# Banded attention in two halves of the heads, with the gate's second half computed between its steps

## The reference

```python
def swa_sink_mixer(x, ln_g, w_in, q_norm_g, sinks, w_out, k_band, v_band, cos, sin):
    h = rmsnorm(x, ln_g)
    q, z = jnp.split(h @ w_in, 2, axis=-1)
    q = partial_rope(rmsnorm(q.reshape(bsz, seq, N_HEADS, HEAD_DIM), q_norm_g), cos, sin)
    ...
    def block_attn(args):                 # one block of 128 queries, keys of it and of the block before
        s = jnp.einsum("bqkgd,bckd->bkgqc", qb, kb) * scale
        s = jnp.where(mask[None, None, None], s, NEG_INF)
        m = jnp.maximum(jnp.max(s, axis=-1, keepdims=True), sink)
        p = jnp.exp(s - m)
        denom = jnp.sum(p, axis=-1, keepdims=True) + jnp.exp(sink - m)
        return jnp.einsum("bkgqc,bckd->bqkgd", p / denom, vb)
    o = lax.map(block_attn, (q, k_band, v_band, jnp.arange(nb)))
    return (o * jax.nn.silu(z)) @ w_out
```

## Time and profile before

| | us |
|---|---|
| median of 3 runs | 1655.44 (1652.76 to 1659.08) |
| the profiled execution | 1645.69, its span 1643.8 |
| PE busy, share of the span | 1356.7, 83% |
| DVE, ACT, POOL busy | 574.7, 416.2, 383.4 |
| mean granted TensorE clock | 0.917 |

### The profile page before, as it was taken

The page is one execution under the profiler, slowest core; times in us unless marked ns, Lnnn a source line. Parts: engine busy times, 40 slices in busy tenths (PEclk is TensorE's granted clock), DMA queues, the critical chain, the costliest instruction groups (busy, mean ns, idle before and its releaser), DMA issues. The chain is left out here.

```text
span 1643.8 us, 16317 instructions
## 1 busy us (share of the span) xinstructions
PE 1356.7 (83%) x6188; PEld 902.0 (55%) x6188; DVE 574.7 (35%) x1069; ACT 416.2 (25%) x787; POOL 383.4 (23%) x241
## 2 busy tenths in 40 slices
PE   3998777698978957968887788783499999999698
PEld 2776554488854753323332333231488887788366
DVE  3749755814024151211111111113531323554652
ACT  4323243415332110000000000002423222433541
POOL 5423222024640012111111111105043432000231
PEclk9999898799989958988998999897799999999799
DMA  7121111223320484999999999997023221332000
GB/s 190 52 103 51 52 52 51 78 77 129 129 76 4 170 341 171 381 409 392 412 407 401 409 377 415 402 413 277 8 95 103 102 94 60 103 102 78 26 20 33
DMA packets 71149, 297.70 MB, mean 181 GB/s; under 512 B 9080, under 2 KB 9128, under 8 KB 50352
## 3 DMA queue, kind: packets, MB, share of 16 engines
q1 hardware_dynamic: 63696, 282.27, 44.6%
q0 software_dynamic: 7392, 14.59, 2.7%
HBM read 292.63 MB, written 12.58 MB: 186 GB/s over the span
## 5 line engine op out<-in xcount | busy, mean ns | idle before, releaser
L688 POOL TENSOR_TENSOR ring_rounded<-ring,ring_rounded 128x2048 fp32r<-128x2048 f32 x54 | 253.3, 4706 | 420.1 <-ACT ring_rounded L1297 419.9
L1033 PE MATMUL bank<-ring,B 128*64 128x512 f32 x992 | 251.4, 665 | 84.5 <-DMA ring<-in_w 83.6
L803 PE MATMUL bank<-HT_rounded,ring_rounded 128*128 128x512 f32 x544 | 217.8, 400 | 5.9 <-DVE ring_rounded L1648 3.3
L805 PE MATMUL bank<-HT_rounded,ring_rounded 128*128 128x512 f32 x544 | 213.6, 393 | 0.0
L804 PE MATMUL bank<-ring_rounded 128*128 128x512 f32 x544 | 213.4, 392 | 0.0
L1033 PEld LDWEIGHTS bank<-ring,B 128*64 128x64 f32 x992 | 85.9, 153 | 226.9 <-issue 225.4
L2000 DVE TENSOR_TENSOR B<-bank,small 128x512 f32<-128x512 f32 x32 | 22.1, 691 | 354.2 <-PE bank L1025 354.2
L1297 ACT ACTIVATE ring_rounded<-ring 128x2048 fp32r<-128x2048 f32 x58 | 110.3, 1915 | 121.5 <-DMA ring<-in_w_in_a 50.6
L805 PE MATMUL bank<-ring_rounded 128*128 128x512 f32 x352 | 138.1, 392 | 0.0
L803 PEld LDWEIGHTS bank<-HT_rounded,ring_rounded 128*128 128x128 f32 x544 | 103.4, 190 | 35.6 <-issue 7.6
L804 PEld LDWEIGHTS bank<-ring_rounded 128*128 128x128 f32 x544 | 103.4, 190 | 22.2 <-issue 1.4
(11 more groups left out here) (355 smaller groups left out, 1917.1 us busy)
## 6 DMA issues: line engine op xcount, KB each, us to landing
ring<-in_w SPq DMA_DIRECT2D x77, 2048.0 KB, 14.9
A<-in_w SPq DMA_DIRECT2D x17, 2048.0 KB, 8.4
ring<-in_w_in_a SPq DMA_DIRECT2D x16, 1024.0 KB, 5.1
ring<-in_w_in SPq DMA_DIRECT2D x14, 1024.0 KB, 7.4
ring<-in_w_in_b SPq DMA_DIRECT2D x8, 1024.0 KB, 5.4
ring<-in_w_out SPq DMA_DIRECT2D x4, 1024.0 KB, 6.2
ring<-in_w_xk SPq DMA_DIRECT2D x4, 1024.0 KB, 5.1
ring<-in_w_xv SPq DMA_DIRECT2D x4, 1024.0 KB, 5.2
```

Of the source, the lines that this page charges most:

```text
L688: pool.tensor_tensor(r32(lo), lo, r32_read(quarter(g, True)), ALU.subtract).then_inc(w_split, 1)
L803: pe.matmul(o, r32(a_hi), r32(b_hi), start=first, stop=False)
L805: return pe.matmul(o, r32(a_lo), r32(b_hi), start=False, stop=last)
L1033: last = pe.matmul(bank[2 + b][64 * j:64 * j + 64, :], xgT[b][:, k, hf, :], w, start=(n == 0), stop=(n == 7), skip_group_check=True)
```

## The change

- The pairs are taken in another order: `window_of(i)` gives the groups 0 and 1 of all four query blocks in steps 0 to 7, groups 2 and 3 in steps 8 to 15.
- zz 4 to 7 leave their place ahead of the loop. One is computed at the end of steps 0, 2, 4 and 6 (`GATE_AT`). Its Silu becomes four operations: ScalarE exp(-z) one step later, behind that step's exponentials; GpSimd adds 1; VectorE, at the head of step i + 2, takes the reciprocal and multiplies by z. That product empties the bank.
- All output blocks come at steps 14 to 18 (one a step) and three after the loop; the last two are computed together in three parts of their rows.
- The splitting of wb1 moves from steps 2 and 3 to 9 and 10, and the chunk zz1 is counted as read when zz 7 is filled.
- The probabilities of the first eight steps lie in other buffers, since hT and lowT are read by zz 4 to 7 until step 6. The low halves of groups 0 and 1 lie in B2.
- The counts of emptied banks follow a list of their own (`emptied`), since VectorE no longer empties in TensorE's order.

```diff
-    uses("act", [("zz", m) for m in range(4, 8)])
+    before = len(closed)
     for i in range(16 + 3):
         if i < 16:
             uses("act", [("ws", i, 0), ("ws", i, 1)])
...
         if i >= 3:
             uses("dve", [("wv", i - 3)])
+        if i in GATE_AT:
+            uses("dve", [("zz", GATE_AT[i])])
         if i in OUT_AT:
             uses("dve", [("wb",) + OUT_AT[i]])
-    uses("dve", [("wb", n, NT - 1) for n in range(2)])
-    return opened, closed, by
-
-
-OUT_AT = {8: (0, 0), 10: (1, 0), 12: (0, 1), 14: (1, 1), 16: (0, 2), 18: (1, 2)}
+    uses("dve", [("wb", 1, 2), ("wb", 0, 3), ("wb", 1, 3)])
+    emptied = closed[:before]
+    for i in range(16 + 4):
+        if i < 16:
+            emptied += [("ws", i, 0), ("ws", i, 1)]
+        if i - 1 in OUT_AT:
+            emptied.append(("wb",) + OUT_AT[i - 1])
+        if i - 2 in GATE_AT:
+            emptied.append(("zz", GATE_AT[i - 2]))
+        if 2 <= i < 18:
+            emptied += [("wp", i - 2, kt) for kt in window_tiles(i - 2)]
+        if 3 <= i < 19:
+            emptied.append(("wv", i - 3))
+    emptied += [("wb", 1, 2), ("wb", 0, 3), ("wb", 1, 3)]
+    return opened, closed, emptied, by
+
+
+GATE_AT = {0: 4, 2: 5, 4: 6, 6: 7}
+OUT_AT = {14: (0, 0), 15: (1, 0), 16: (0, 1), 17: (1, 1), 18: (0, 2)}
+
+
+def window_of(i):
+
+    if i < 8:
+        return i // 2, i % 2
+    return i // 2 - 4, 2 + i % 2
...
-            add_chunk(f"zz{n}", w_cols(w_b, D + 512 * n), V, ("zz", 4 * n + 3))
+            add_chunk(f"zz{n}", w_cols(w_b, D + 512 * n), V, ("zz", 4 * n + 3), n == 0)
...
+                if j in GATE_AT:
+                    m = GATE_AT[j]
+                    pool.wait_ge(sem("z_exp_ready"), m - 3)
+                    pool.tensor_scalar(zT[:, m, :], zT[:, m, :], 1.0, None, ALU.add).then_inc(sem("z_sum_ready"), 1)
...
-            to_cols("zz1", V, [("zz", m) for m in range(4, 8)], hT, lowT)
...
+                if i in GATE_AT:
+                    m = GATE_AT[i]
+                    w = chunk("zz1")
+                    split_gemm(fill(V, "zz", m)[:, :], lambda k: w(k, P * (m - 4), P * (m - 3)), cols)
                 if i in OUT_AT:
                     out_block(*OUT_AT[i])
-            for n in range(2):
-                out_block(n, NT - 1)
+            out_block(1, 2)
+            outs = [fill(V, "wb", n, NT - 1)[:, :] for n in range(2)]
+            parts = [chunk(f"wb{n}") for n in range(2)]
+            for k0, k1, rows in ((0, 4, 8), (4, 6, 15), (6, 8, 16)):
+                pe.wait_ge(sem("y3_low_ready"), rows)
...
-            for m in range(4, 8):
-                o = filled(V["zz", m])
-                act.activation(zT[:, m, :], o[:, :], ACT.Silu).then_inc(done, 1)
...
+                if i - 1 in GATE_AT:
+                    m = GATE_AT[i - 1]
+                    o = filled(V["zz", m])
+                    act.activation(zT[:, m, :], o[:, :], ACT.Exp, scale=-1.0).then_inc(sem("z_exp_ready"), 1)
+                if i in (9, 10):
+                    high_half("wb1", i - 9)
...
+                if i - 2 in GATE_AT:
+                    m = GATE_AT[i - 2]
+                    o = filled(V["zz", m])
+                    dve.wait_ge(sem("z_sum_ready"), m - 3)
+                    own(dve.reciprocal(zT[:, m, :], zT[:, m, :]))
+                    dve.tensor_tensor(zT[:, m, :], o[:, :], zT[:, m, :], ALU.mult).then_inc(done, 1)
```

More of the change, by code:

```diff
@@ L177, in second_plan @@
     opened, by = [what for what, _ in plan], dict(plan)
-    closed = list(opened)
+    closed, emptied = list(opened), []
     def uses(engine, whats, opens=True, closes=True):
@@ L234, in __init__, with number @@
         self.emptied = of_engine
-def number(opened, closed, by, base, act0, dve0):
-    assert sorted(map(str, opened)) == sorted(map(str, closed))
+def number(opened, closed, order, by, base, act0, dve0):
+    assert sorted(map(str, opened)) == sorted(map(str, closed)) == sorted(map(str, order))
     count, emptied = {"act": act0, "dve": dve0}, {}
-    for what in closed:
+    for what in order:
         count[by[what]] += 1
@@ L266, in build @@
     order1 = [what for what, _ in plan1]
-    U, act1, dve1 = number(order1, order1, dict(plan1), 0, 0, 0)
+    U, act1, dve1 = number(order1, order1, order1, dict(plan1), 0, 0, 0)
     V, _, _ = number(*second_plan(), n1, act1, dve1)
@@ L299, in build @@
         B1 = sb("B1", NT * HEADS * (P + 1))
-        B2 = sb("B2", NT * SEQ)
+        B2 = region("B2", NT * SEQ)
         E = region("E", NT * SEQ)
@@ L452, in build, with wS, window_low, window_high @@
         q2T, zT = f3(A0, (KD, SEQ)), f3(A1, (KD, SEQ))
-        wS = f3(HT, (3, 4, 2 * P))
+        wS_first = [f3(XN, (4, 2 * P), 2048), f3(XN, (4, 2 * P), 3072), f3(B0, (4, 2 * P))]
+        wS_second = [f3(HT, (4, 2 * P), 1024 * n) for n in range(3)]
+        low3 = f3(B2, (4, SEQ))
+        def wS(i):
+            return (wS_first if i < 8 else wS_second)[i % 3]
+        def window_low(j):
+            nb, g = window_of(j)
+            if g < 2:
+                return low3[:, 2 * g:2 * g + 2, P * nb:P * nb + P]
+            return lowT[:, 2 * g:2 * g + 2, P * nb:P * nb + P]
+        def window_high(j):
+            nb, g = window_of(j)
+            return yT2[:, 2 * g:2 * g + 2, P * nb:P * nb + P]
         wpT = f3(E, (2, 2, 4 * P))
@@ L1199, in _, with out_rows @@
             pe.wait_ge(sem("mask16_ready"), 1)
+            def out_rows(k, t):
+                return yT2[:, k, P * t:P * t + P], (low3 if k < 4 else lowT)[:, k, P * t:P * t + P]
             def out_block(n, t):
@@ L1204, in out_block @@
                 w = chunk(f"wb{n}")
-                pe.wait_ge(sem("y3_low_ready"), 4 * t + 4)
-                split_gemm(o, lambda k: (yT2[:, k, P * t:P * t + P], lowT[:, k, P * t:P * t + P]), w)
+                pe.wait_ge(sem("y3_low_ready"), 2 * t + 10)
+                split_gemm(o, lambda k: out_rows(k, t), w)
             for i in range(16 + 3):
                 if i < 16:
-                    nb, g = divmod(i, WKV)
+                    nb, g = window_of(i)
                     k0, n = (P * (nb - 1), 2 * P) if nb else (0, P)
@@ L1225, in _ @@
                     j = i - 2
-                    nb, g = divmod(j, WKV)
+                    nb, g = window_of(j)
                     pe.wait_ge(sem("wp_ready"), j + 1)
@@ L1231, in _ @@
                             c0 = P * (kt - (nb == 0))
-                            last = pe.transpose(o[:, P * q:P * q + P], wS[:, j % 3, q, c0:c0 + P], ident)
+                            last = pe.transpose(o[:, P * q:P * q + P], wS(j)[:, q, c0:c0 + P], ident)
                         last.then_inc(bank_filled, 1)
@@ L1247, in _ @@
                     last.then_inc(bank_filled, 1)
+                if i in GATE_AT:
+                    m = GATE_AT[i]
+                    w = chunk("zz1")
+                    split_gemm(fill(V, "zz", m)[:, :], lambda k: w(k, P * (m - 4), P * (m - 3)), cols)
                 if i in OUT_AT:
                     out_block(*OUT_AT[i])
-            for n in range(2):
-                out_block(n, NT - 1)
+            out_block(1, 2)
[3 more added lines that the diff above has]
+                pe.wait_ge(sem("y3_low_ready"), rows)
+                for n, o in enumerate(outs):
+                    for k in range(k0, k1):
+                        last = passes(o, lambda k: out_rows(k, NT - 1), parts[n], k, k == 0, k == KD - 1)
+                    if k1 == KD:
+                        last.then_inc(bank_filled, 1)
         @block.scalar
@@ L1589, in _ @@
                             c = 8 * (i % 2) + q
-                            last = act.activation(wS[:, i % 3, q, 0:n], o[:, n * pr:n * pr + n], ACT.Exp,
+                            last = act.activation(wS(i)[:, q, 0:n], o[:, n * pr:n * pr + n], ACT.Exp,
                                                   bias=neg[:, c:c + 1], scale=WD ** -0.5, accum_out=zsum[:, c:c + 1])
@@ L1594, in _ @@
                     act.activation(stat[:, 16 + c:20 + c], stat[:, c:c + 4], ACT.Exp).then_inc(sem("w_exp_ready"), 1)
-                if i in (2, 3):
-                    high_half("wb1", i - 2)
-                if 6 <= i < 18:
+                if i - 1 in GATE_AT:
[4 more added lines that the diff above has]
+                    high_half("wb1", i - 9)
+                if 2 <= i < 18 and 0 in window_tiles(i - 2):
                     j = i - 2
@@ L2208, in low_of @@
             def low_of(j):
-                nb, g = divmod(j, WKV)
                 wait_high()
-                v = lambda t: t[:, 2 * g:2 * g + 2, P * nb:P * nb + P]
-                dve.tensor_tensor(r32(v(lowT)), v(lowT), r32_read(v(yT2)), ALU.subtract).then_inc(sem("y3_low_ready"), 1)
+                v = window_low(j)
+                dve.tensor_tensor(r32(v), v, r32_read(window_high(j)), ALU.subtract).then_inc(sem("y3_low_ready"), 1)
             def add_out(n, t):
@@ L2235, in _ @@
```

(15 more changed lines are left out.)

12 lines of the change are left out of this document (5 added, 7 removed).

## The result

The changed kernel takes 1677.04 us (median of 4 runs, 1676.41 to 1678.89), the kernel before 1656.05 in the runs beside it: a ratio of 1.0127, 95% interval 1.0096 to 1.0158. The change makes the kernel slower by 21 us.

A forecast was written before the change was run, and what follows sets the result against it. Steps 0 to 7 were held by a ring of VectorE and ScalarE that leaves TensorE holes. Chained step times put the first output block at 1607.5 against a break-even of 1587.4: +20 on 1655.4, 1675.5 us; range 1656 to 1689.

The forecast's parts named there:

- The start: Step 0: its maximum comes only after wb0's second half is split, until 1503.8, and is done at 1505.0.
- The addition: GpSimd's addition of 1 in each gate: taken as 0.85 us, at most 0.95.
- The bank: Steps 4, 6 and 8: transposes wait 4 to 6 us for VectorE's gate product to free the PSUM bank; pairs 17 to 20 us.
- C: Rival: the bank doesn't hold, the ring alone sets 14.4 us a pair; T = 1594, +6.5 us, 1662; 10 in 100.
- T: Start of output block (0,0): forecast 1607.5, 20 us above the 1587.4 below which the change wins; last matmul 53.3 us later.
- The clock: Half clock behind two long waits, steps 4 and 6: 2 us apiece, bounds 0 and 5 for both together.
- D: Rival: the half clock stays in steps 4 to 13, gate blocks and first output block wholly at 0.50; +30 us, 1685; 12 in 100.
- Step 8: First of the steps from 8 on, with exponentials over 128 columns: listed at 6.0 us.
- Steps 9 and 10: Steps carrying the two halves of wb1, moved from steps 2 and 3: 9.2 and 9.5 us.
- The other side: Rival A: gates as cover fill the holes of steps 0 to 7; 6.6 us faster, 1649; 12 in 100.
- A: Rival: early product, TensorE sets pairs of 13 us or less, holes of steps 0 to 7 filled; 6.6 us faster, 1649; 12 in 100.

The follow-up runs named there:

- e2: Changed kernel, but ScalarE copies z out of its bank right behind the exponential and VectorE's product reads the copy; ratio 1.0049 to the kernel before.
- e6: Changed kernel with a two-operation tanh gate, tanh ahead of step i + 1's exponentials and product ahead of its maximum; ratio 0.9991 to the kernel before.
- e8: e6's gate in steps 0 to 3, old order of pairs and output blocks, wb1 split in steps 5 to 7; ratio 0.9928 to the kernel before.
- e9: e6 with wb1's halves split apart in steps 8 to 10, order by halves of the heads kept; ratio 0.9941 to the kernel before.
- e10: Changed kernel with only wb1's split moved: ScalarE's halves at the end of steps 8 and 9, VectorE's in 9 and 10; ratio 1.0088 to the kernel before.

## Why the prediction was right

The forecast was +20 us and 1675.5; measured +21.0 in the medians, +21.5 in the last stretch. Point by point, with the trace's times less 11.7 for the later start:

- *The start.* Maximum of step 0 forecast 1505.0, measured 1516.5 - 11.7 = 1504.8.
- *The addition.* A mis-sized term: 0.85 forecast, at most 0.95 allowed, 1.49 measured. An operation with one operand on GpSimd is slower here than the one with two on as many columns (1.04). It cost some 0.6 us in step 2 and in step 4, and 0.4 in steps 6 and 8, where it ran beside ScalarE's copies.
- *The bank.* Waits of 4 to 6 us in steps 4, 6 and 8, put down to the product: measured 5.43, 6.57 and 7.21, so the last two are longer than the text allowed. Pairs of 17 to 20 us: measured 20.0 and 20.7 with the clock's share, as against 19.7 and 20.2 in the forecast's own list. e2 and e6 show that it was the bank and its place in the order. C is out; its T should have been 1596.4 by the list's own terms (1528.8 + 2 x 14.4 + 38.8), not 1594.
- *The clock.* 2 us for each of the two waits. Behind the second the trace has 3.7 us at 0.50 for what takes 2.05, so 1.65, and 0.16 more in the gate block; behind the first 1.0 and 0.7. D, a half clock that stays through gate and output blocks, did not come: the gate block at 1564.4 and the first output block ran at 1.00, and the mean from step 4 to the end of step 11 is 0.81 (TensorE is busy for 44.5 of 73.7 us there, where D had less than half).

```profile
1532.30:1606.00 73.70, 44.50 (x242) 27.78 (x240) 40.68 (x78) 25.48 (x90) 17.93 (x11) 0.81 0.08 29
```

- *Step 8.* The other mis-sized term: 6.0 forecast, without saying from what, 4.7 measured. At the maximum of step 8 the forecast was 2.5 us early (70.1 against 72.6 from the end of the q transposes), most of it the addition; this step gave 1.3 of them back. That is luck.
- *Steps 9 and 10.* 9.2 and 9.5 forecast, 9.1 and 9.5 measured. T, relative: 108.9 forecast, 109.9 measured; behind it 53.3 forecast, 53.6 measured.
- *The other side.* A wanted the pairs at 13 us. With the chain cut (e6) they are 15.1 and 12.8, and the kernel is then level with the one before, not 6.6 us faster: A's price was too hopeful as well.

The sum met the result because each part was a chain, counted in the order of the engines' queues, and the mechanism was the one forecast; that it came within 1.5 us took, besides, two errors that cancelled in part. The sum of busy times would have said that VectorE, busy for 61.9 of the 145.2 us of the last stretch before, had room for 16 us more.

## What to carry to other kernels

When a piece of work moves between the steps of a loop, count which buffer it holds and which instruction gives it back. Here, with eight banks, the eighth use behind it waits for that instruction if it is late, and everything that it waits for comes into series. The same two instructions cost 8 us more at the head of step i + 2 than ahead of the maximum of step i + 1. Place work where its engine waits: 1.9 us of ScalarE and 2.3 of VectorE per half of weights made a step 4 us longer or more between exponentials and division (9.1 and 9.5 us against some 5), and 1.4 (e8) or 0.5 us (e9, e10) at the end of the step.

## What the runs showed of the hardware

VectorE's operation on two SBUF operands all but stood still here while GpSimd's multiplication ran. In e8 the split of a half chunk, 2.29 us alone, took 3.28 both times that it met a division; it ended 2.14 us behind GpSimd's end (1555.18 and 1557.32 here):

```profile
1553.28 1.90 POOL L818 TENSOR_TENSOR B<-B,small 128x1024 f32<-128x1024 f32 x1 [2.57 <-DVE small L2300]
```
```profile
1553.12 0.67 DVE L2306 COPY E<-bank 128x512 f32<-128x512 f32 x1
1553.71 0.41 DVE L2313 SCALAR_TENSOR_TENSOR ring<-bank,A 128x256 f32<-128x256 f32 x1
1554.04 3.28 DVE L2172 TENSOR_TENSOR ring_rounded<-ring,ring_rounded 128x2048 fp32r<-128x2048 f32 x1
```

The copy out of PSUM and the product of a bank with one SBUF operand, in the same 1.90 us, kept their 0.67 and 0.41. The 1.0 us more is most of the 1.4 us that a half cost in e8. In e9 the split met only the last 0.28 us of a division and took 2.43; it ended 2.15 us behind it. The short low half (128x256, 0.42 us alone) shows the same: in the twelve profiles it took 0.56, 0.99, 1.08 or 1.4 us where it began 0.28, 0.71, 0.80 or 1.13 us ahead of the multiplication's end, and always ended 0.28 us behind it. Beside GpSimd's addition, which has one operand, it kept its 0.42 us all eight times, as here in the changed kernel:

```profile
1554.89 1.49 POOL L825 TENSOR_SCALAR A<-A 128x512 f32<-128x512 f32 x1 [0.42 <-ACT A L1654]
```
```profile
1555.62 0.42 DVE L2271 TENSOR_TENSOR B_rounded<-B,XN_rounded 128x256 fp32r<-128x256 f32 x1 [2.21 <-ACT XN_rounded L1633]
```

The Trainium skill, "GPSIMD Engine Reference", Specifications, says that GpSimd shares its SBUF interfaces with VectorE and contends with instructions that have two SBUF inputs; the trace agrees for the multiplication, with 1.0 us, and shows no contention beside the one-operand addition. What was not tried: the same with the split ahead of the division.
